# A two-block transformer kernel: the mLSTM's running maximum in the rounded type, and the first two product groups of a stage computed side by side

## The reference, cut to what matters

```python
for l in range(DEPTH):                       # 2 layers
    u = x * (1.0 + sc1) + sh1
    ...  # u @ w_in + b_in is cut into conv, qkv, o, gates of the mLSTM, low-rank q and kv, branch gates
    y_conv = conformer_conv(a, w_dw, b_dw, cn_g, cn_b, w_conv_out)
    h_x, _, _ = mlstm_bidir(q_x, k_x, v_x, fwd_x, bwd_x, st_f, st_b)
    y_ml = mlstm_out(h_x, o_pre, ml_g, w_ml_out)
    y = gated_merge(gates, y_conv, y_ml, o_x @ w_mla_out, w_out, b_out)
    x = layer_norm(alpha * x + g1 * y, ln1_g[l], ln1_b[l])
    x = layer_norm(alpha * x + g2 * sq_relu_mlp(x * (1.0 + sc2) + sh2, w1[l], b1[l], w2[l], b2[l]), ...)

def mlstm_chunkwise(...):                    # per chunk of 128 tokens, forward and backward, 4 heads
    log_d = jnp.where(causal, bcum[..., :, None] - bcum[..., None, :] + li[..., None, :], -jnp.inf)
    m_row = jnp.maximum(inter, jnp.max(log_d, -1))
    s = jnp.einsum('bhld,bhsd->bhls', qf, kf) * jnp.exp(log_d - m_row[..., None])
    ...
```

## Time and profile before

| what | value |
|---|---|
| time, median of 3 runs | 3446.89 us (3442.93 to 3458.04) |
| the profiled execution's own time | 3444.87 us |
| its span, first to last instruction | 3443.1 us |
| PE busy, share of the span | 3287.2 us, 95% |
| DVE, ACT, POOL busy | 1832.5, 1190.8, 1105.0 us |
| mean granted TensorE clock | 0.98 of full speed |

### The profile page before, as it was taken

One profiled execution on the slowest core, in us unless ns is written; L12 is line 12 of the kernel. 1 busy time (PEld: TensorE's weight loads), 2 busy tenths in 40 slices (PEclk: granted clock), 3 DMA queues, 4 the chain that ended last, 5 costly groups with the idle time before them and its releaser, 6 DMA issues. The chain is left out here.

```text
span 3443.1 us, 50669 instructions
## 1 busy us (share of the span) xinstructions
PE 3287.2 (95%) x19144; PEld 2673.1 (78%) x19144; DVE 1832.5 (53%) x2750; ACT 1190.8 (35%) x1791; POOL 1105.0 (32%) x553
## 2 busy tenths in 40 slices
PE   5999999899999999999899999998999979999998
PEld 4888667788888888887777667787888857788886
DVE  2869444613268243246886455228433577677634
ACT  2233334532244222123442435334332364422223
POOL 2433000332233232223341013443444434344442
PEclk8999999999999999999999999999999989999999
DMA  6222154022221222222222341332333222233332
GB/s 183 62 60 57 45 158 143 7 65 58 61 68 57 67 62 62 62 62 62 72 74 52 107 115 34 89 97 78 90 97 92 87 66 62 74 92 95 92 96 78
DMA packets 549134, 270.18 MB, mean 78 GB/s; under 512 B 55922, under 2 KB 547146, under 8 KB 548827
## 3 DMA queue, kind: packets, MB, share of 16 engines
q1 hardware_dynamic: 547330, 267.20, 27.5%
q10 hardware_dynamic: 889, 0.30, 0.0%
q0 software_dynamic: 736, 0.17, 0.0%
HBM read 265.50 MB, written 2.10 MB: 78 GB/s over the span
## 5 line engine op out<-in xcount | busy, mean ns | idle before, releaser
L374 POOL TENSOR_TENSOR weights_low<-weight_ring,weights_high 128x1024 fp32r<-128x1024 f32 (+1 forms) x408 | 977.2, 2396 | 1765.1 <-ACT weights_high L365 1764.8
L365 ACT ACTIVATE weights_high<-weight_ring 128x1024 fp32r<-128x1024 f32 (+1 forms) x408 | 410.1, 1006 | 1176.9 <-PE ps L475 1142.8
L470 PE MATMUL ps<-features_high,weights_high 128*128 128x512 f32 (+1 forms) x1552 | 500.1, 341 | 16.4 <-DVE features_low L852 14.0
L471 PE MATMUL ps<-features_low,weights_high 128*128 128x512 f32 (+1 forms) x1552 | 495.4, 341 | 0.0
L470 PE MATMUL ps<-u_high,weights_high 128*128 128x512 f32 (+2 forms) x944 | 368.8, 394 | 24.0 <-DVEq L1135 8.0
L471 PE MATMUL ps<-u_low,weights_high 128*128 128x512 f32 (+2 forms) x944 | 362.8, 388 | 0.0
L470 PEld LDWEIGHTS ps<-features_high,weights_high 128*128 128x128 f32 x1552 | 293.8, 189 | 59.7 <-issue 11.1
L471 PEld LDWEIGHTS ps<-features_low,weights_high 128*128 128x128 f32 x1552 | 293.7, 189 | 37.2
L1223 DVE SCALAR_TENSOR_TENSOR conv<-conv,vectors 128x512 f32<-128x512 f32 x360 | 291.0, 858 | 31.2 <-DVE conv L1223 28.9
L470 PE MATMUL ps<-mlp_u_high,weights_high 128*128 128x512 f32 (+3 forms) x1024 | 288.1, 311 | 10.7 <-DVE mlp_u_low L2912 7.4
L475 PE MATMUL ps<-features_high,weights_low 128*128 128x512 f32 (+1 forms) x1552 | 287.8, 336 | 0.0
(11 more groups left out here) (627 smaller groups left out, 5366.4 us busy)
## 6 DMA issues: line engine op xcount, KB each, us to landing
weight_ring<-in_w_in SPq DMA_DIRECT2D x262, 256.0 KB, 3.2
weight_ring<-in_w SPq DMA_DIRECT2D x256, 256.0 KB, 3.0
weight_ring<-in_w_mod SPq DMA_DIRECT2D x192, 256.0 KB, 3.8
weight_ring<-in_w_up SPq DMA_DIRECT2D x88, 256.0 KB, 3.1
weight_ring<-in_w_out SPq DMA_DIRECT2D x48, 256.0 KB, 3.1
weight_ring<-in_w_down SPq DMA_DIRECT2D x32, 256.0 KB, 3.1
weight_ring<-in_w_mla_out SPq DMA_DIRECT2D x32, 128.0 KB, 2.3
weight_ring<-in_w_conv_out SPq DMA_DIRECT2D x32, 128.0 KB, 2.3
```

The costliest lines, as they stand in the source:

```text
L365: act.activation(core.ring_high[:, split_slot(run, q), 0:n], core.ring[:, slot, 0:n], ACT.Copy).then_inc(core.high_ready.sem, 1)
L374: core.nc.gpsimd.tensor_tensor(core.ring_low[:, split_slot(run, q), 0:n], core.ring[:, (run.first + q) % SLOTS, 0:n], high.bitcast(F32), A ...
L470: pe.matmul(to, w_high[:, k, 0:m], high(k, a, b), start=(first and k == ks[0]), stop=False, skip_group_check=True)
L471: pe.matmul(to, w_high[:, k, 0:m], low(k, a, b), start=False, stop=False, skip_group_check=True)
```

## The change

The maximum's scan (L1195) writes its result as fp32r; ACT's copies of it lie in a tile of that type of its own, a 36x128 block of ones in the same type is made by one more DVE instruction per layer, and the matmul L1848 takes these two. The first two groups of layer 0's projection, of every branch of both merges and of both MLPs are computed by `paired_products`; in the merges the first round stands ahead of the loop for that, and for the conv branch both gated heads are waited for before it. In the MLP the sums stand after k = 4 of the pair. Waits for operands stand only in the first product that needs them. In the second block the low part (L766) is made before the squares, the sum of squares goes into (feed-forward) or ahead of (last stage) the second product instead of the first, and the loop over the down projection's two halves is written out.

```diff
-def paired_products(core, pe, run, q, uses, f, high, low, width, ready, kts=KT):
+def paired_products(core, pe, run, q, use, f, high, low, ready, width=T, cuts=None, between=None):
...
+    pe.wait_ge(core.high_ready.sem, n[0])
+    pe.wait_ge(core.tile_free[f].sem, core.tile_free[f].at(use + 1))
+    for k in range(KT):
         ready(k)
...
+        with_high(0, k)
+        if k == 0:
+            pe.wait_ge(core.split_ready.sem, n[0])
+        mm = with_low(0, k)
+        if k == KT - 1:
+            mm.then_inc(core.weights_used.sem, 1)
+        if k == 0:
+            pe.wait_ge(core.high_ready.sem, n[1])
+            pe.wait_ge(core.tile_free[f + 1].sem, core.tile_free[f + 1].at(use + 1))
+        with_high(1, k)
+        if between is not None and k in between:
+            between[k]()
     pe.wait_ge(core.split_ready.sem, n[1])
...
+    for k in range(KT):
+        mm = with_low(1, k)
     mm.then_inc(core.weights_used.sem, 1)
...
-            if seam is None or n > 1:
-                product(core, pe, *group(name, g), n // 2, n % 2, high, low, width=tokens(name, g),
-                        m=QH if name == "small" else P, ready=ready if n == 0 else None)
-            elif n == 0:
-                paired_products(core, pe, runs["conv"], 0, 0, 0, high, low, wx, lambda k: seam.wait_features(pe, 0, k))
+            if n == 0:
+                paired_products(core, pe, runs["conv"], 0, 0, 0, high, low, ready, width=wx)
+            elif n > 1:
...
-                    k = row(nc.vector.tensor_tensor_scan(back(maximum[rd[d], chunks(c)], d), back(rows[rd[d], G, chunks(c)], d),
+                    k = row(nc.vector.tensor_tensor_scan(back(maximum[rd[d], chunks(c)].bitcast(F32R), d), back(rows[rd[d], G, chunks(c)], d),
...
-    maxima = core.free[:, 0:4 * T].rearrange("p (h t) -> p h t", t=T)
+    maxima, ones = core.maxima.rearrange("p (h t) -> p h t", t=T), core.round_ones
...
-            pe.matmul(above, core.ones[rd[d], :], maxima[rd[d], :, chunks(c)], start=False, stop=True, skip_group_check=True)\
+            pe.matmul(above, ones[rd[d], :], maxima[rd[d], :, chunks(c)], start=False, stop=True, skip_group_check=True)\
...
+        nc.vector.tensor_copy(ones[gates.both, :], core.ones[gates.both, :]).then_inc(s["picks_ready"].sem, 1)
...
-            with pe.Fori(0, 4) as i:
+            if b == 1:
                 for f in range(2):
-                    if b == 1:
-                        pe.wait_ge(h_gated.sem, h_gated.at(3 + f))
-                    product(core, pe, run, i, f, 4 * b + i, f, high, low, width=w, ready=ready if b == 0 else None)
+                    pe.wait_ge(h_gated.sem, h_gated.at(3 + f))
...
+            paired_products(core, pe, run, 0, 4 * b, 0, high, low, ready, width=w)
+            for f in range(2):
+                product(core, pe, run, 0, 2 + f, 4 * b, 2 + f, y_high, y_low, kts=4, width=w, ready=None if f else branch_ready)
+            with pe.Fori(1, 4) as i:
...
+SUMS_AFTER = 4
...
-            for q in range(KT):
-                product(core, pe, run, i, q, use(i, q), q % 2, high, low, cuts=cuts, between=sums if i == q == 0 else None,
-                        ready=lambda k: pe.wait_ge(s["u_split"].sem, s["u_split"].at(k + 1)))
+            if i == 0:
+                paired_products(core, pe, run, 0, use(0, 0), 0, high, low, lambda k: pe.wait_ge(s["u_split"].sem, s["u_split"].at(k + 1)),
+                                cuts=cuts, between={SUMS_AFTER: sums})
+            for q in range(0 if i else 2, KT):
+                product(core, pe, run, i, q, use(i, q), q % 2, high, low, cuts=cuts)
...
             dve.wait_ge(free[k % 2].sem, free[k % 2].at(k // 2 + 2))
+            following.gain_low(dve, x(k), gain(k), k, TX)
             squares.add(x(k), k)
-            following.gain_low(dve, x(k), gain(k), k, TX)
...
-                    between=(lambda: scale.sum(pe)) if q == 0 else None)
+                    between=(lambda: scale.sum(pe)) if q == 1 else None)
...
-                product(core, pe, run, i, f, i, f, high, low, width=TX, between=sum_and_turn if i == f == 0 else None,
+                if i == 0 and f == 1:
+                    sum_and_turn()
+                product(core, pe, run, i, f, i, f, high, low, width=TX,
```

More of the change, by code:

```diff
@@ new lines, in paired_products, with with_high @@
+    outs = [bank(core, 2 * (f + g), 1024) for g in range(2)]
+    cuts = cuts or [(a, b, a) for a, b in parts(width)]
+    weights = [[w[:, split_slot(run, q + g), :].rearrange("p (k c) -> p k c", c=P) for w in (core.ring_high, core.ring_low)]
+               for g in range(2)]
+    def with_high(g, k):
+        for a, b, at in cuts:
+            to = outs[g][:, at:at + b - a]
+            pe.matmul(to, weights[g][0][:, k, :], high(k, a, b), start=(k == 0), stop=False, skip_group_check=True)
+            pe.matmul(to, weights[g][0][:, k, :], low(k, a, b), start=False, stop=False, skip_group_check=True)
@@ new lines, in with_low @@
+    def with_low(g, k):
+        for a, b, at in cuts:
+            mm = pe.matmul(outs[g][:, at:at + b - a], weights[g][1][:, k, :], high(k, a, b), start=False, stop=(k == KT - 1),
+                           skip_group_check=True)
+        return mm
+    pe.wait_ge(core.high_ready.sem, n[0])
+    pe.wait_ge(core.tile_free[f].sem, core.tile_free[f].at(use + 1))
+    for k in range(KT):
+        ready(k)
+        with_high(0, k)
[10 more added lines that the diff above has]
+            between[k]()
@@ L516, in paired_products @@
     pe.wait_ge(core.split_ready.sem, n[1])
-    for k in range(kts):
-        for a, b in parts(width):
-            mm = pe.matmul(outs[1][:, a:b], parts_of[1][1][:, k], high(k, a, b), start=False, stop=(k == kts - 1), skip_group_check=True)
+    for k in range(KT):
+        mm = with_low(1, k)
     mm.then_inc(core.weights_used.sem, 1)
@@ L2766, in _ @@
                 for q in range(KT):
-                    product(core, pe, run, i, KT + q, use(i, KT + q), q % 2, *hidden, width=w, late=0 if q else 2, ready=hidden_ready)
+                    product(core, pe, run, i, KT + q, use(i, KT + q), q % 2, *hidden, width=w, late=0 if q else 2, ready=None if q else hidden_ready)
                 continue
@@ L3816, in _, with acted_ready @@
                 product(core, pe, run, i, q, i, q, high, low, width=TX)
-        with pe.Fori(0, 2) as i:
+        for i in range(2):
             for q in range(12):
                 part = q % 3
-                def acted_ready(k, part=part):
+                def acted_ready(k):
                     pe.wait_ge(low_made.sem, low_made.at(3 + 8 * part + k))
@@ L3826, in _ @@
                         lambda k, a, b: acted_low[:, 8 * part + k, a:b], kts=(8, 8, 6)[part], width=TX,
-                        first=(part == 0), last=(part == 2), ready=acted_ready if q < 3 else None)
+                        first=(part == 0), last=(part == 2), ready=acted_ready if i == 0 and q < 3 else None)
     @block.scalar
```

47 lines of the change are left out of this document (20 added, 27 removed).

## The result

The changed kernel takes 3427.7 us (median of 5 runs, 3426.9 to 3432.4) against 3448.4 us (median of 5, 3442.9 to 3458.0) in the same session: a ratio of 0.9941, 95% interval 0.9928 to 0.9955, or 20.7 us faster. Predicted were 3427 us, between 3414 and 3441. Its profiled execution took 3427.4 us with a span of 3425.6, 17.5 less than the span before, where the prediction's sum was 17.8.

What follows compares the result with a forecast made beforehand. PE, busy 95% of the span, was taken as the bound. Terms 11.7 + 8.0 - 2.4 - 1.6 + 0.8 + 1.3 = 17.8 us took the profiled 3444.9 to 3427.1, forecast as 3427 us, range 3414 to 3441.

Steps and rivals of the forecast that it cites:

- The maximum: mLSTM scores of both layers: rounded maximum's matmul becomes one pass, 0.6 us saved on each of 20 scores, 11.7 us net.
- the 0.3 that I took off for DVE: mLSTM steps with statistics: DVE, with some 1.1 us more work, is level with PE, so 12.0 becomes 11.7 us.
- Pairs where features arrive: Layer-0 projection and both merges: five units per arriving tile instead of two, PE hardly waits; 2.7 + 3.7 + 1.6 = 8.0 us gained.
- Only the stretch at the lower clock remains: Paired products: slow-clock stretch of 6 us in layer 0 (3.0 lost), about 5 in layer 1 (2.5 lost).
- What the pairs cost: Later merge branches: conv waits for both gated heads (1.7 us together), mLSTM branch loses 0.2 and 0.5; -2.4 us.
- MLP l0: Layer 0's MLP: idle time moves ahead of the third product and grows, clock may fall; -1.6 us, between -0.25 and -2.8.
- MLP l1: Layer 1's MLP: norm chain starts about 1.3 us earlier, clock falls before the third product; +0.8 us (0 to 1.6).
- The second block: Feed-forward's start: low part ahead of squares, third product 2.7 us earlier if the clock holds, 0 if it falls; +1.3 us taken.
- The 0.5 for the output projection's later eviction: Second block's output projection: later eviction of the first tile gives 0.5 us back, set against the last stage's gain.
- the last stage's 0.6: Last stage: its 1.7 us wait shrinks by about 0.6, netted to zero with the output projection's 0.5.
- Waits and loops: Waits only at first products and loops written out: nothing gained, since products with satisfied waits take the same 5.60 us.
- the clock: Slower rival, chance 0.05: new holes bring 1.2 GHz stretches costing 3.0 us each; six more than counted eat the gain.

## Why the prediction was right

**The maximum**: 12.3 us for 11.7. The mechanism was right, the gap around the matmul stayed, and the 0.3 that I took off for DVE in the steps with statistics was not there: 0.62 us in each of the 12 steps.

**Pairs where features arrive**: 11.2 us for 8.0, the term most mis-sized. "Only the stretch at the lower clock remains, 6 us in layer 0" was the step that was off: once PE has five units for each tile the stretch behind the first tile costs 1.5 us on top of 16.8 in layer 0's merge (18.3) and 2.3 in its projection, not 3.0, and 1.6 instead of 2.5 in layer 1. I had taken its length from a row in which PE stood waiting within it.

**What the pairs cost**: 2.5 us for 2.4; undoing them gave 2.9 back. The wait at the conv branch grew by 0.8 and 0.5 instead of 1.0 and 0.7, the mLSTM branch lost 0.4 and 0.9 for 0.2 and 0.5.

**MLP l0**: -1.2 us for -1.6. The third product started 0.24 us later for 0.25, and the clock fell. The run without the pair shows that I had credited the old arrangement with a clock that it doesn't always have. **MLP l1**: +1.1 for +0.8, and 2.1 in the run that undoes the pair; the wait of 2.43 us for the second group's high weights was not foreseen and didn't show in the stage's time.

**The second block**: +1.3 was forecast, and 0 for the places around it; measured were -0.2 from the feed-forward's start up to and with the last stage's shorter wait (0.96 for 1.71 us), and -0.6 in the output projection. The wait that takes the place of the old one was foreseen (third product waiting for ACT's weights behind the scale chain). Counted from the feed-forward's first product the third started 2.3 us earlier for 2.7, since the sum ended 1.1 us later than before, not 0.6, and the clock behind the hole took 2.7 us: the end of my range that I had called 0. Another 0.5 us went in the output projection, a product every 5.62 us instead of 5.49, at the pace of DVE's new order (5.49 again in the run that undoes it). The 0.5 for the output projection's later eviction was right (0.6), but the last stage's 0.6 that I had set against it brought nothing in the sum.

**Waits and loops**: nothing, as far as products without waits keep their 5.60 us; this part was not tried by itself.

**What I had no term for**: the program's start (-0.8) and the clock at places that the change doesn't touch (-1.5, +0.2, +2.2, -1.3 and -1.3), together -2.5 us. Terms that were too small (pairs 3.2, MLPs 0.7, maximum 0.6), one that was too large (second block, 2.1) and these cancel, so that 17.8 met 17.5. The total's closeness is partly luck. Of the rivals, "the clock" was right in kind: the changed kernel has new stretches behind its new holes, but it lost others, and with 55.4 against 56.0 us over the whole it is far from the six more that would have made it slower. Why the clock falls behind a hole in one trace and not in the next stays open.

## What to carry to other kernels

When the first product of a stage waits for tiles that come one by one, two products side by side take away the waits between tiles (11.2 us over three places against the trace before, 13.6 against the run that undoes them); where all operands are there already, the pair only asks earlier for the second group's weights and evictions and costs half a microsecond each. When you take a wait away, find out which queue the next one stands in: here the gain lay not in the order of DVE, which only exchanged 3.39 for 3.30 us, but in ACT making weights ahead of a chain that was itself waiting. And before crediting a term of a microsecond or two to an edit, look whether a stretch at 1.2 GHz stands there in one trace and not in the other, and take a second trace of the same kernel.

## What the runs showed of the hardware

The clock can fall with PE never idle: behind some 3 us of matmuls of 36 rows with 36 columns and 4 rows with 6 columns it was 0.52 in the changed kernel and 0.53 in the run of the maximum alone, and 1.00 in the trace before; of fourteen traces twelve have the stretch. The same idle time (3.49 us, 3.30, 2.96) was followed by 1.00 in one trace and by 0.5 to 0.7 in another, and the stretches cost between 1.7 and 5 us each. Keeping PE busy with thrown-away work in holes of 3.3 to 6.8 us gave a clock of 1.00 behind all fourteen that were filled; in three of them (layer 1's merge, in each run with fillers) it fell while that work ran. A matmul of 128 columns that is not rounded is executed as two instructions of 0.12 us. And the DVE instruction held by POOL's low parts is simply the next one: 1.37 us for the low part (0.74 before) and then 2.88 for the square. The Trainium skill's page "SBUF — State Buffer", section "Who interferes with whom", says that a DVE instruction with two SBUF inputs contends with a GpSimd instruction that reads SBUF; both instructions have two, and the trace agrees.
